# Samples' products moved into the scans, and a unit's last tiles computed inside it: a two-layer hybrid decoder step on one core

## The reference

```python
o = qd_c @ S + (qk_c) @ v_c
S = S * decay + kd_c^T @ v_c
```

## Time and profile before

| | |
|---|---|
| median of 3 runs | 2837.93 us |
| profiled execution | 2838.67 us |
| its span, first to last instruction | 2836.9 us |
| TensorE busy | 2752.9 us, 97% |
| VectorE busy | 1560.6 us, 55% |
| ScalarE busy | 429.1 us, 15% |
| mean granted clock | 0.986 |
| HBM traffic | 52 GB/s |

### The profile page before, as it was taken

How to read it: one execution, slowest core, us unless ns; L and a number is a source line. 1 busy time by engine, 2 the same in 40 slices (tenths; PEclk the granted TensorE clock), 3 DMA queues, 4 the chain that set the end, 5 groups by cost and what they waited for, 6 DMA issues and landing times.

```text
span 2836.9 us, 41615 instructions
## 1 busy us (share of the span) xinstructions
PE 2752.9 (97%) x17386; PEld 2663.7 (94%) x17386; DVE 1560.6 (55%) x2890; ACT 429.1 (15%) x868; POOL 0.2 (0%) x4
## 2 busy tenths in 40 slices
PE   7999999999999999999999999999999999999998
PEld 7888888899899999999999999998899999999998
DVE  7656657555776346264466534436576254363563
ACT  4433514222330000000001112122230000000001
POOL 0000000000000000000000000000000000000000
PEclk9999999999999999999999999999999999999999
DMA  3010101111211111111112111012301111111121
GB/s 129 23 39 16 39 24 45 46 53 46 105 64 45 45 45 48 49 45 45 46 52 90 60 53 62 30 62 69 114 31 53 45 45 49 49 45 45 46 66 60
DMA packets 44986, 150.94 MB, mean 53 GB/s; under 512 B 6024, under 2 KB 11016, under 8 KB 43792
## 3 DMA queue, kind: packets, MB, share of 16 engines
q1 hardware_dynamic: 33984, 115.42, 12.3%
q10 hardware_dynamic: 10832, 32.99, 3.2%
HBM read 130.32 MB, written 18.08 MB: 52 GB/s over the span
## 4 chain that ended last, share of the span: by engine, by line
PE 88%; DVE 8%; ACT 2%; issue 1%; DMA 1%; DVEq 0%; ACTq 0%; SPq 0%
PE proj L350 71%; PE bank L421 9%; PE proj L693 3%; PE bank L418 1%; PE bank L408 1%; DVE s L843 1%; DVE w_lo L799 1%; DVE w_hi L796 1%; PE bank L373 0%; PE proj L373 0%; PE bank L660 0%; DVE s L1069 0%; DVE s L965 0%; DVE x_lo L891 0%; DVE x_lo L889 0%
## 5 line engine op out<-in xcount | busy, mean ns | idle before, releaser
L350 PE MATMUL proj<-x_hi,w_hi 128*128 128x344 f32 x4572 | 1503.9, 329 | 29.5 <-DVE s L843 16.9
L350 PE MATMUL proj<-x_hi,w_lo 128*128 128x344 f32 x4572 | 1471.0, 322 | 0.0
L350 PE MATMUL proj<-x_lo,w_hi 128*128 128x344 f32 x4572 | 1470.6, 322 | 0.0
L350 PEld LDWEIGHTS proj<-x_hi,w_hi 128*128 128x128 f32 x4572 | 869.3, 190 | 51.2 <-issue 18.1
L350 PEld LDWEIGHTS proj<-x_lo,w_hi 128*128 128x128 f32 x4572 | 869.9, 190 | 2.6
L350 PEld LDWEIGHTS proj<-x_hi,w_lo 128*128 128x128 f32 x4572 | 869.0, 190 | 0.0
L1341 DVE TENSOR_TENSOR h<-h,proj 128x344 f32<-128x344 f32 x144 | 73.8, 512 | 372.3 <-PE proj L350 372.3
L799 DVE TENSOR_TENSOR w_lo<-w_raw,w_hi 128x1024 fp32r<-128x1024 f32 x195 | 239.0, 1226 | 8.1 <-DVE state L1115 1.4
L1326 DVE TENSOR_TENSOR mlp_t<-proj,rbc 128x344 f32<-128x344 f32 x192 | 99.0, 516 | 237.6 <-PE proj L350 224.0
L421 PE MATMUL bank<-s,s 128*128 128x128 f32 x1088 | 139.6, 279 | 13.6 <-DVE s L1011 4.2
L421 PEld LDWEIGHTS bank<-s,s 128*128 128x128 f32 x1088 | 128.0, 192 | 23.4 <-DVEq L777 6.6
(11 more groups left out here) (324 smaller groups left out, 2031.9 us busy)
## 6 DMA issues: line engine op xcount, KB each, us to landing
w_raw<-w_all SPq DMA_DIRECT2D x204, 512.0 KB, 3.5
h<-x SPq DMA_DIRECT2D x8, 516.0 KB, 9.2
h<-x ACTq DMA_DIRECT2D x8, 516.0 KB, 6.4
h_spill<-h ACTq DMA_DIRECT2D x8, 516.0 KB, 2.6
h<-h_spill ACTq DMA_DIRECT2D x8, 516.0 KB, 5.6
y<-h SPq DMA_DIRECT2D x24, 172.0 KB, 1.9
sample_C<-state_c ACTq DMA_DIRECT2D x4, 1024.0 KB, 6.6
s_state_c<-sample_C ACTq DMA_DIRECT2D x4, 1024.0 KB
```

The costliest lines, as they stand in the source:

```text
L350: last = nc.tensor.matmul(PJ[:, tt, 0:TT], w[slot][:, k, :], x[:, k, tt * TT:(tt + 1) * TT], start=(at == 0 and j == 0), stop=(at == len(o ...
```

## The change

Three tables and the order of the tiles change, and with them what each place carries:

1. *First chunk.* The scans' products with the zero state are left out: k*S and q*S in delta's chunk 0, q*S in retention's and mLSTM's. The state's first value is a copy of the chunk's product in place of memset and update; the wait for the stores of the unit before moves there. Delta's chunk 0 multiplies the inverse with V directly, with no "residual".
2. *Samples.* The place "sample" is gone. Chunk c of each scan does the product(s) of sample c: in delta between the inverse's product and "values", elsewhere behind the chunk's products. VectorE prepares the samples' k and q before the scan (in delta inside the level chain, in retention before "operands"). In a chunk the state's product now comes before the output's.
3. *mLSTM after the scan.* VectorE's small instructions on samples are reordered and done for both value halves at once; a place "drains" lets it drain thirds behind "rows". ScalarE does the output gate's tanh before chunk 6 and not before the scan.
4. *Late tiles.* `LATE = (1, 2)`: the last tile of a layer-0 unit (v) and the last two of a layer-1 unit (now the output gates) are computed as the first fill of the unit itself. Before unit 0 only 3 (4) tiles are computed. VectorE waits for the late tiles at the places that use them (before the levels; before "operands"; after chunk 3 of mLSTM).
5. *Handovers by thirds.* In a layer's last unit the late tiles come first in the filler, then the output projection. x_hi is written third by third, each when the last late tile's same third is computed (layer 0: all behind the rotary copies; layer 1: before chunks 0, 2 and 4). x_lo follows in VectorE's stream by `hand`: in layer 0 after "rope q", before "operands" and inside "operands"; in layer 1 three k-chunks of a third after each of chunks 1 to 6. TensorE waits for x third by third (`by_third`). `out_partial` on TensorE still waits first until the last projection tile is drained.
6. *Start of layer 0.* Constants and the memset stand before the wait for ScalarE; the split of tile 4, the drains of tile 3 and the next split (`for _ in first`) move behind the gate columns.

The diff, cut to its core:

```diff
-PARTIAL = ((3, 0, 1, 2), (4, 5, 2, 3))
+LATE = (1, 2)
+PARTIAL = ((3, 0, 1, 2), (2, 3, 4, 5))
...
               "level 0": 0, "level 1": 0, "block": 0, "turn": 0, "scan": 1, "state": 2, "residual": 1, "values": 1,
-              "sample": 2, "rows": 5, "output": 10, "outer": 10}
+              "rows": 7, "output": 10, "outer": 11}
 RETENTION_FILL = {"gate": 5, "rope q": 10, "rope k": 10, "operands": 10, "scan": 8,
-                  "state": 4, "sample": 4, "rows": 5, "outer": 3, "output": 5}
-RETENTION_LAST_FILL = {**RETENTION_FILL, "state": 2, "output": 6}
-MLSTM_FILL = {"start": 14, "operands": 12, "scan": 10, "state": 5, "sample": 8, "rows": 9, "sum": 8,
-              "outer": 8, "output": 12}
-MLSTM_LAST_FILL = {"start": 8, "operands": 8, "scan": 4, "state": 3, "sample": 4, "rows": 6, "sum": 4,
-                   "outer": 3, "output": 6}
...
+                  "state": 4, "rows": 7, "outer": 4, "output": 6}
+RETENTION_LAST_FILL = {**RETENTION_FILL, "rope k": 12, "state": 3, "output": 6}
+MLSTM_FILL = {"start": 14, "operands": 12, "scan": 10, "state": 5, "rows": 14, "drains": 0, "sum": 10,
+              "outer": 8, "output": 13}
+MLSTM_LAST_FILL = {**MLSTM_FILL, "state": 4, "rows": 11, "sum": 8, "outer": 6, "output": 10}
...
+SHORT_STEPS = ("rows",)
...
-                            pe.wait_ge(x_ready, ready + 3 * at + tt + 1)
+                            pe.wait_ge(x_ready, ready + (len(order) * tt + at if by_third else 3 * at + tt) + 1)
...
+                def sample_product(b):
...
+                    if b == 0:
+                        pe.wait_ge(state_in, n.awaited(state_in, 16)[1])
+                        claim(4, "dve")
+                    mm(MB[4][:, 2 * b:2 * b + 2], s[9][:, b * P:(b + 1) * P], kq[:, b, :])
...
-                    if delta:
+                    if delta and c:
                         claim(0, "dve")
                         publish(mm(MB[0][:, 0:P], chunk(k, c), S[:, 0:P]), 0)
                     claim(2, "act")
-                    mm(MB[2][:, 0:C], S[:, 0:P], chunk(qg, c), True, False)
+                    if c:
+                        mm(MB[2][:, 0:C], S[:, 0:P], chunk(qg, c), True, False)
                     if delta:
-                        yield "residual"
-                        pe.wait_ge(*n.awaited(to_pe))
...
+                            yield "residual"
+                            pe.wait_ge(*n.awaited(to_pe))
                         claim(1, "dve")
-                        publish(mm(MB[1][:, 0:P], chunk(s[15], c), resid[:]), 1)
+                        publish(mm(MB[1][:, 0:P], chunk(s[15], c), resid[:] if c else chunk(V, 0)), 1)
+                        sample_product(c)
                         yield "values"
...
                     vv = vnew[:] if delta else chunk(V, c)
-                    publish(mm(MB[2][:, 0:C], vv, chunk(QKT, c), False, True), 2)
                     claim(3, "dve")
                     publish(mm(MB[3][:, 0:P], chunk(Kd, c), vv), 3)
...
+                    publish(mm(MB[2][:, 0:C], vv, chunk(QKT, c), c == 0, True), 2)
+                    if not delta:
+                        sample_product(c)
...
-                    mm(MB[c % 2][:, 0:2 * P + 1], chunk(qw, c), S[:], True, False)
+                    if c:
+                        mm(MB[c % 2][:, 0:2 * P + 1], chunk(qw, c), S[:], True, False)
                     claim(3, "dve")
                     publish(mm(MB[3][:, 0:2 * P + 1], chunk(Kd, c), v_tok[:, c, :]), 3)
-                    publish(mm(MB[c % 2][:, 0:2 * P + 1], chunk(QKW, c), v_tok[:, c, :], False, True), c % 2)
...
+                    publish(mm(MB[c % 2][:, 0:2 * P + 1], chunk(QKW, c), v_tok[:, c, :], c == 0, True), c % 2)
+                    if c == 0:
+                        pe.wait_ge(state_in, n.awaited(state_in, 16)[1])
+                        claim(4, "dve")
                     for j in range(2):
-                        mm(MB[4][:, j * NB + b:j * NB + b + 1], ss_c[:, b, j * P:(j + 1) * P], samp[:, b:b + 1])
+                        mm(MB[4][:, j * NB + c:j * NB + c + 1], ss_c[:, c, j * P:(j + 1) * P], samp[:, c:c + 1])
...
+                yield from projections(t0 - LATE[layer], LATE[layer], X)
                 pe.wait_ge(proj_drained, 3 * t0 + 3)
                 pe.sem_inc(proj_full, 3)
                 for j in range(4):
                     t = t0 + 1 + j
                     yield from tile_steps(t, w_slot(t), X, ready if j == 0 else None,
-                                          order=IN_TURN[:KC - KTAIL[layer]])
+                                          order=IN_TURN[:KC - KTAIL[layer]], by_third=True)
...
-                following = (projections(T_AB + 4 * u + 4, 4, XA) if u < 2 * HEADS - 1
+                following = (projections(T_AB + 4 * u + 4 - LATE[0], 4, XA) if u < 2 * HEADS - 1
...
                     drain(t, tt, f)
+                if t + 1 in TAILS:
+                    all_drained(t)
+                    v.sem_inc(proj_drained, 3)
...
...
+                def due():
+                    return steps // KC if steps < KC * NT * late else NT * late + (steps - KC * NT * late) // per
...
                     if place in SHORT_STEPS:
                         continue
-                    if thirds == steps // per and ahead is PIECE:
...
-                    while thirds < steps // per and ahead:
+                    while thirds < due() and ahead:
                         thirds += ahead is THIRD
                         ahead = next(following, None)
...
+            def out_start(layer, X, tt, chunks=None):
+                for c in chunks or range(KC - KTAIL[layer]):
                     v.wait_ge(*n.awaited(mix_hi))
-                    for tt in range(NT):
-                        low_of_mix(layer, X, c, tt)
+                    low_of_mix(layer, X, c, tt)
...
+                late = LATE[layer]
+                yield from projections(s, *((T_AB, 8 * HEADS - late, 8 * HEADS, 4) if layer == 0 else
+                                            (T_C, 6 * HEADS - late, 6 * HEADS, 6)))
...
+                def samples_of(q, k):
+                    nc.vector.tensor_copy(kq[:, :, 0], k[:, SEQ:TOK])
+                    nc.vector.tensor_copy(kq[:, :, 1], q[:, SEQ:TOK])
+                    tt_(sm[0], q[:, SEQ:TOK], k[:, SEQ:TOK], ALU.mult)
...
+                        if hand and x == 0:
+                            hand(0)
+                    all_drained(T_AB + 4 * unit + 3)
                     nc.vector.tensor_copy(samp[:, 0:NB], s[2][:, SEQ:TOK])
+                    samples_of(s[6], s[7])
...
+                    if hand:
+                        hand(1)
...
+                    if hand:
+                        hand(2)
...
+                    all_drained(T_AB + 4 * unit + 3)
...
+                        if lv == 5:
+                            samples_of(q, k)
...
-                nc.vector.memset(S[:, 0:P], 0.0).then_inc(*n.made(to_pe))
+                tell(to_pe)
...
-                    if delta:
+                    if delta and c:
                         ps = take(0)
                         stt(resid[:], ps[:, 0:P], negbe[:, c, h:h + 1], chunk(s[17], c), ALU.mult, ALU.add).then_inc(*done(0))
                         tell(to_pe)
                         yield "residual"
+                    if delta:
                         ps = take(1)
                         nc.vector.tensor_copy(vnew[:], ps[:, 0:P]).then_inc(*done(1))
...
                         yield "values"
                     ps = take(3)
                     gl = s[7][:, c * C + C - 1:c * C + C] if delta else consts[:, K_RG + 4 + h:K_RG + 5 + h]
-                    stt(S[:, 0:P], S[:, 0:P], gl, ps[:, 0:P], ALU.mult, ALU.add).then_inc(*done(3))
+                    if c:
+                        stt(S[:, 0:P], S[:, 0:P], gl, ps[:, 0:P], ALU.mult, ALU.add).then_inc(*done(3))
+                    else:
+                        if unit:
+                            v.wait_ge(stored, n.awaited(stored, 32)[1])
+                        nc.vector.tensor_copy(S[:, 0:P], ps[:, 0:P]).then_inc(*done(3))
                     n.settle()
                     if c < NC_ - 1:
                         tell(to_pe)
                         yield "state"
...
-                yield "sample"
...
+                        stt(S[:], S[:], s[6][:, c * C + C - 1:c * C + C], ps[:, 0:2 * P + 1], ALU.mult, ALU.add).then_inc(*done(3))
+                    else:
+                        if h:
+                            v.wait_ge(stored, n.awaited(stored, 64)[1])
+                        nc.vector.tensor_copy(S[:], ps[:, 0:2 * P + 1]).then_inc(*done(3))
                     n.settle()
                     if c < NC_ - 1:
...
+                    if c == 3:
+                        all_drained(T_C + 6 * h + 5)
+                        tell(to_act)
+                    if hand and 0 < c < NC_ - 1:
+                        hand(c - 1)
+                ps = take(4)
+                step(nc.vector.tensor_copy(small[:, 4 * NB:8 * NB], ps[:, 0:4 * NB]))
```

(38 more changed lines are left out.)

162 lines of the change are left out of this document (62 added, 100 removed).

## The result

The changed kernel takes 2787.58 us (median of 4 runs, 2784.94 to 2791.71) against 2838.15 (4 runs, 2836.71 to 2839.72): ratio 0.9823, 95% interval 0.9806 to 0.984. That is 50.6 us, 1.8%, less; 2790 was forecast. The profiled execution has a span of 2785.9 us at a mean clock of 0.992, against 2836.9 at 0.986.

The account below looks back on a forecast made before the run. TensorE, busy 97% of the span, was taken as the bound, so time comes from its work, idle gaps or clock. Terms summed to 48.3 us off 2838.67, giving 2790.4, forecast 2790 us for the median; range 2774 to 2812.

Parts of the forecast that it names:

- First chunk and samples' products: Delta units: zero-state products dropped 0.9 us, samples' block absorbed in the scan 1.6, each unit; net 8.4, plus mLSTM 1.8.
- Clock behind the blocks: Half clocks behind the samples' blocks go with them: 5.1 us in delta units, 6.8 in mLSTM units 0 to 2.
- Start of layer 0: Before unit 0: one tile fewer and VectorE's new order bring the first fill step to 63.3; 7.0 us gained (3 to 10).
- Retention handover: Last retention unit: TensorE idles 7.8 us for the late tile's drain; 11.2 lost against 9.9, so -1.3 us (-7 to +6).
- mLSTM's waits: mLSTM units 0 to 2: waits of 1.4 us each for VectorE's drain go, 4.3 us gained.
- Last mLSTM unit: Handover by thirds there recovers 8.2 us of 9.0 lost; the unit's other waits 4.6 and two half clocks 3.4.
- a window under 9.5 us: Sign for the mLSTM handover: third unit's end to "operands" of the last mLSTM unit under 9.5 us, clock 1.00.
- Rest of that unit: Last mLSTM unit after its handover: of waits 2.8, 1.7 and 1.3 us, 4.6 gained; two of three low stretches go, 3.4.
- A: Rival: the clock doesn't come back, narrow work isn't the cause or lows appear elsewhere; 2805 us, chance 0.14.
- B: Rival: both handovers wait, mLSTM's for a drained late tile too, and retention's goes to -7; 2806 us, chance 0.12.
- C: Rival: retention's handover is hidden because VectorE drains sooner, and the start gives 10; 2780 us, chance 0.12.
- D: Rival: narrow products in every chunk of all 12 scans bring the half clock; slower, up to 2886 us, chance 0.04.

Follow-up runs that it names:

- e1: Changed kernel with the samples' products as one block behind each scan again; 2806.2 us, +18.6 against the changed kernel.
- e2: Changed kernel with the products with the zero first state, the state's memset and the first residual put back; 2795.8 us, +8.2.
- e4: Changed kernel with three tiles before unit 0 but VectorE's old order at the start; 2798.4 us, +10.9.
- e3: Changed kernel without a late tile in layer 0: four tiles before unit 0, old start order, old whole-chunk retention handover; 2796.0 us, +8.4.
- r1: Changed kernel with the retention handover's late-tile drains and all low parts behind "rope q", 53 fill steps before "operands" instead of 37; 2783.6 us, -4.0.
- e6: Changed kernel without the place "drains" in VectorE's stream of the mLSTM units, TensorE's fill as changed; 2790.9 us, +3.3.
- r2: Changed kernel with retention fill 8, 8, 9 instead of 5, 10, 10, so VectorE drains a third before "rope q"; 2784.1 us, -3.5.
- r3: Changed kernel with 4 instead of 10 fill steps at each "output" of the last mLSTM unit, 17 left behind it instead of 5; 2781.7 us, -5.9.
- r4: Changed kernel with r1, r2 and r3 together; 2778.2 us, -9.3, ratio to the kernel before 0.9788.

## Why the prediction was right

- **First chunk and samples' products.** Forecast 2.5 us a delta unit, measured about 2.8 to 3.0 (1.8 by e1, 1.0 by e2, and 0.2 of the later chunks' 20.74 us, which the sum had not). The term was low because I let 0.2 us of the block stay, left out that the state's product now comes sooner, and charged VectorE's three small instructions in the level chain 0.25 us a unit; from the chain's first product to its end the two traces differ by less than 0.05 us. Delta unit 2 had also a wait of 1.6 us for a drain before, which I had not seen and which fell to 0.2. mLSTM and retention: 0.45 and 0.2 a unit by e2, as forecast.
- **Clock behind the blocks.** Right, and shown by e1: the products are the same, only packed. By the rule of the Trainium skill cited in the prediction (idle gaps between bursts lose the clock, in "TensorE: Matmul & The Clock Gate", "Why this matters for your kernels") e1 would have been 2794 us; it is 2806. That gaps cost the clock too is as true here (in the 8.4 us gap of the retention handover a stretch of 10.2 us at 0.50 begins and lasts 5.2 us past it), but they are not the only thing. Three stretches of 3.4 us were given back elsewhere: one in delta unit 1's start (169.7), and one each at layer 1's start (1610.1) and at the tail of w_out_a (777.3), where 6.8 us at 0.50 stand in place of 3.4. The first is new in kind: in front of it stand no wait and no block of samples' products with the state, but four outer products of 8 rows and the row products. In the twelve traces with the change it, or one like it, stands at 16 of the 36 starts of delta units 1 to 3, before at none of three. Traces with and without it differ by 0.6 us at that place, not by the 1.7 that half of it would be, so I had left out a place where the clock falls, but a cheap one.
- **Start of layer 0.** 10.6 against 7.0, just above the upper bound of 10. Of the 10.6, 0.7 lie ahead of the first norm sum at 32 us, where both kernels do the same (there the traces with this start differ by up to 1.3 among themselves), so 9.9 belong to the change. The first fill step comes at 62.23, not 63.3, and no half clock followed, where I had put one. Of ten traces of kernels with this start three have it (within 62.8 to 66.5), and with it the stretch from unit 0's first to its second row products takes 1.3 to 1.4 us more; that much of the term is chance of the clock. The size, not the mechanism, was off: e4 shows the order of VectorE's stream to be most of it.
- **Retention handover.** Followed queue by queue: a wait of 7.8 us forecast, 8.4 found, at the same record and with the same releaser; -1.3 forecast, -1.3 found up to "operands" and -1.8 up to the norm sum, -1.3 between the two handovers in e3. It is a part of the change that costs, and r1 mends it.
- **mLSTM's waits.** They went, but mostly by the shifted fill (e6).
- **Last mLSTM unit.** 13.4 against 16.7, the one term that was too high. The handover gave 9.3, more than the 8.2. The sign that I had set for it, a window under 9.5 us, didn't come and couldn't: I had left the 17 fill steps of before in it, the new table puts 26 there, and they take the 12.45 us, all busy. "Rest of that unit", 4.6 + 3.4, gave about 3.6: the waits of 1.3 and 1.7 us went, the last (2.8, 2.7 after) stayed with its half clock, in this trace 6.8 us at 0.50 in place of 3.4 (without it, as in r2's trace, the term would have been 2.8 higher). I had counted five left-over steps as cover; VectorE does a split and two drains of that very fill before the low parts, so what counts is the distance to TensorE's end. The 17 steps of r3 are enough; nothing between 5 and 17 was run.
- **Rivals.** A fell (e1), though lows did appear elsewhere; B half came (the retention handover waits, the mLSTM one doesn't), C fell, D fell: all scans of after are at 1.00. The errors, +3.6, +4.0, -0.5, -1.2, -3.3, cancel to 2.6 us. That the total was nearer than its parts is luck.

## What to carry to other kernels

Work too small to fill TensorE did the least harm strewn between wide matmuls, most of all in front of a wait that exists anyway: in the delta scan it cost nothing, in a block it cost its own 1.8 us and in most cases the clock behind it. When a step is to come earlier, look at what stands between it and its input on the *other* engine; at this kernel's start the order there was worth 7.8 us on top of the 2.8 of the moved tile. Fill spent where nothing waits is missing at the last wait of a stage (r3). And before a gain of a few us is put down to an edit, look in the trace whether it lies in the stretch that was edited: r2's median was right and its reason was not.

## What the hardware showed

- A block of samples' products (in a delta unit 18 records, 16 of them of two columns, 1.80 us with TensorE busy all the time) is followed by a half clock in 6 of 8 cases of the delta and mLSTM units in e1 and 7 of 8 before (an mLSTM block has 32 records). With the same products one by one, none of the 12 scans after has one in it or right behind it, nor has any scan of the other ten traces with strewn products. Why the retention blocks, of the same form as delta's, had none in four cases before and four in e1 is open; so a block is not enough by itself.
- The half clock isn't settled by the kernel alone: behind the same wait of 2.0 us it came in r4 (713.5) and didn't in r1. A stretch is 3.4 to 13.7 us long. It costs about half of that where TensorE has work enough (3.4 us cost 1.4 at 63.1 in e6 and 1.5 at 1580.8 in r1), less where TensorE idles in it (the 10.2 us at 698.7 hold 5.15 us of work) or at a delta unit's start (0.6). A few such chances in the layers' seams are of the size of the runs' spread (2784.9 to 2791.7); that they make up the spread is not shown, as each kernel has one trace. One of them, at 713.5, is 3.2 of the 4.1 us by which r4 missed the sum of the single gains.
